# One core of a hybrid streaming encoder step: value chunks, gate sums, weight loads and the first output tiles moved between stages of the even layer

## What is computed

```python
def even_layer(...):
    h = rmsnorm(x, g_pre)
    proj = jnp.einsum('bld,de->ble', h, w_in)
    u, v, za, zb, xbc, dt_raw = jnp.split(proj, EVEN_SPLITS, axis=-1)
    ya, v_rows = gmlp_branch(u, v, za, ws, bs, gv)         # silu(z) * gelu(u) * (W @ rmsnorm(gelu(v)) + b)
    yb, s_fin, new_ctx = ssd_branch(zb, xbc, dt_raw, ...)  # Mamba-2 scan, silu(zb) gate, rmsnorm over 2 groups
    o = jnp.einsum('ble,ed->bld', jnp.concatenate([ya, yb], axis=-1), w_out)
    return x + rmsnorm(o, g_post), v_rows, s_fin, new_ctx
```

## Time and profile before

| | us |
|---|---|
| median of 3 runs | 1649.04 (1648.13 to 1650.0) |
| the profiled execution, device time | 1649.58 |
| its span | 1647.8 |
| PE busy | 1573.0 (95%) |
| PE weight loads busy | 1448.2 (88%) |
| DVE, ACT, POOL busy | 795.8 (48%), 664.1 (40%), 439.5 (27%) |
| DMA | 121.08 MB, 73 GB/s over the span |
| TensorE granted clock, mean | 0.989 |

### The profile page before, as it was taken

One profiled execution on the slowest core, in us unless ns is written; L12 is line 12 of the kernel. 1 busy time (PEld: TensorE's weight loads), 2 busy tenths in 40 slices (PEclk: granted clock), 3 DMA queues, 4 the chain that ended last, 5 costly groups with the idle time before them and its releaser, 6 DMA issues.

```text
span 1647.8 us, 26614 instructions
## 1 busy us (share of the span) xinstructions
PE 1573.0 (95%) x9539; PEld 1448.2 (88%) x9539; DVE 795.8 (48%) x1752; ACT 664.1 (40%) x1241; POOL 439.5 (27%) x267
## 2 busy tenths in 40 slices
PE   6999999998999999999998899999999999998898
PEld 5999999998999999888887888889888889887676
DVE  5547776674883412236475533443344343435432
ACT  6433332331233323335455344544454544445321
POOL 1214543442211112144342221312221221215000
PEclk9999999999999999999999899999999999999999
DMA  4122232112102111154454446624142423213121
GB/s 147 41 67 70 58 92 64 56 44 78 42 13 68 39 38 40 49 179 153 166 177 135 59 73 43 64 53 67 33 71 45 65 39 64 58 42 134 52 90 71
DMA packets 129221, 121.08 MB, mean 73 GB/s; under 512 B 10074, under 2 KB 112996, under 8 KB 129164
## 3 DMA queue, kind: packets, MB, share of 16 engines
q1 hardware_dynamic: 129164, 120.31, 29.9%
HBM read 101.63 MB, written 18.66 MB: 73 GB/s over the span
## 4 chain that ended last, share of the span: by engine, by line
PE 82%; DVE 6%; issue 5%; ACT 5%; DMA 1%; POOL 1%; ACTq 0%; SPq 0%; DVEq 0%; POOLq 0%
PE PB L727 77%; PE PB L731 5%; DVE NRML L1850 2%; ACT L1290 1%; ACT L1736 1%; ACT NRMH L1284 1%; DVE SB L1854 0%; ACT SB L1813 0%; DMA nf_rows<-NFROW 0%; ACT WH L1284 0%; POOL WL L612 0%; ACT PT L1284 0%; ACT SQJ L1324 0%; DVE XT L1857 0%; DVE KALL L1857 0%
## 5 line engine op out<-in xcount | busy, mean ns | idle before, releaser
L727 PE MATMUL PB<-HH,WH 128*128 128x352 f32 x1872 | 621.3, 332 | 8.5 <-ACT VG L1304 4.3
L727 PE MATMUL PB<-HH,WL 128*128 128x352 f32 x1872 | 604.1, 323 | 0.0
L727 PE MATMUL PB<-HL,WH 128*128 128x352 f32 x1872 | 603.5, 322 | 0.0
L727 PEld LDWEIGHTS PB<-HH,WH 128*128 128x128 f32 x1872 | 354.2, 189 | 22.7 <-issue 13.9
L727 PEld LDWEIGHTS PB<-HL,WH 128*128 128x128 f32 x1872 | 355.3, 190 | 0.0
L727 PEld LDWEIGHTS PB<-HH,WL 128*128 128x128 f32 x1872 | 353.8, 189 | 0.0
L612 POOL TENSOR_TENSOR WL<-WRAW,WH 128x1024 fp32r<-128x1024 f32 x82 | 200.2, 2441 | 552.4 <-ACT WH L1284 544.8
L1284 ACT ACTIVATE WH<-WRAW 128x1024 fp32r<-128x1024 f32 x112 | 117.9, 1053 | 28.1 <-DMA WRAW<-in_w_in_even_dram 19.2
L1813 ACT ACTIVATE SB<-SB,small 128x128 f32<-128x128 f32 (+8 forms) x72 | 53.8, 748 | 80.5 <-DVE small L1854 80.5
L1850 DVE TENSOR_TENSOR Y<-PB,Y 128x128 f32 (+2 forms) x72 | 20.2, 280 | 132.5 <-PE PB L727 132.5
L727 PE MATMUL PB<-PT,VTOK 128*128 128x128 f32 (+2 forms) x624 | 81.7, 274 | 0.1
(11 more groups left out here) (299 smaller groups left out, 2396.8 us busy)
## 6 DMA issues: line engine op xcount, KB each, us to landing
WRAW<-in_w_out_even_dram SPq DMA_DIRECT2D x48, 512.0 KB, 3.5
WRAW<-in_w_in_even_dram SPq DMA_DIRECT2D x44, 512.0 KB, 3.8
WRAW<-in_w_in_odd_dram SPq DMA_DIRECT2D x32, 512.0 KB, 8.1
ACSB<-acs_rows SPq DMA_DIRECT2D x16, 528.0 KB, 4.8
NFB<-nf_rows SPq DMA_DIRECT2D x8, 656.0 KB, 3.8
XS<-in_x_prompt_dram SPq DMA_DIRECT2D x8, 512.0 KB, 7.1
XT<-in_x_prompt_dram SPq DMA_DIRECT2D x8, 512.0 KB, 5.2
x_rows<-OG SPq DMA_DIRECT2D x8, 512.0 KB, 5.4
```

What stands on the lines that cost most here:

```text
L727: return pe.matmul(out, lhsT, rhs, start=start, stop=stop)
```

## The change

Four parts, all in the even layer:

- **The last pair.** PE projects a chunk in steps 0, 1, 3 and 5: the three of value tile 21, then the first of tile 22. ACT reads tile 21's chunks (`read_v`) within the pair and makes the high part of tile 23 there. Of the two remaining chunks of tile 22 one stands ahead of the turn of `CST`, one behind it. SP loads tiles 23 and 24 ahead of the store of `CSO`.
- **Tiles 31 and 32** are loaded ahead of the wait for `V` and the store of its sample rows.
- **The gate sums** go two by two behind the three chunks of tile 32, into banks 6 and 7 by turns; the copy of `VS` for the next spatial product moves ahead of their reads on DVE.
- **The first output tiles.** ACT's `prepare(0)` and `prepare(1)` stand ahead of the reads of the last two tiles (43 and 44), DVE's `lows(0)` and `lows(1)` ahead of the last `gated`.

```diff
@@ SP
+        for j in range(2):
+            load_w(tile_no(W_V + 2 + j, 1, 0), even(D + P * j + 2 * P))
         sp.wait_ge(S("cso"), 1)
...
-        with sp.Fori(1, 4) as i:
+        with sp.Fori(2, 4) as i:
             for j in range(2):
                 load_w(tile_no(W_V + j, 2, i), even(D + P * j + 2 * P * i))
         load_w(tile_no(W_UZ, 1, 0), even(0))
         load_w(tile_no(W_UZ, 1, 1), even(2 * D))
+        load_w(tile_no(W_UZ + 2, 1, 0), even(P))
+        load_w(tile_no(W_UZ + 3, 1, 0), even(2 * D + P))
         sp.wait_ge(S("v_normed"), 4)
...
-        with sp.Fori(1, 8) as t:
+        with sp.Fori(2, 8) as t:
@@ PE, pair_steps
-                elif i in (1, 3, 5):
-                    project_chunk(tile_no(W_V, 1, 0), tile_no(W_V, 1, 0), i // 2, HH, HL)
+                elif i in (0, 1, 3):
+                    project_chunk(tile_no(W_V, 1, 0), tile_no(W_V, 1, 0), (0, 1, 1, 2)[i], HH, HL)
+                elif i == 5:
+                    project_chunk(tile_no(W_V + 1, 1, 0), tile_no(W_V + 1, 1, 0), 0, HH, HL)
@@ PE, v_group
-        pe.wait_ge(S("yf"), 24)
-        turn(PB[3][0:6 * XBC_TILES, 0:P], CST[:, :, :].rearrange("p r t -> p (r t)")).then_inc(S("cst_turn"), 1)
-
...
-            if not isinstance(i, int):
+            if isinstance(i, int):
+                project_chunk(vt[1], vt[1], 1, HH, HL)
+                pe.wait_ge(S("yf"), 24)
+                turn(PB[3][0:6 * XBC_TILES, 0:P], CST[:, :, :].rearrange("p r t -> p (r t)")) \
+                    .then_inc(S("cst_turn"), 1)
+                project_chunk(vt[1], vt[1], 2, HH, HL)
+            else:
                 project(vt[0], vt[0], HH, HL)
-            project(vt[1], vt[1], HH, HL)
+                project(vt[1], vt[1], HH, HL)
@@ PE, the gate sums
-        project_uz(0, 1)
-
-        pe.wait_ge(S("s_read"), 3)
-        for n in range(6):
-            g, c = n // 3, n % 3
-            pe.wait_ge(S("y_sq"), 4 + 4 * g)
-            if n == 5:
-                pe.wait_ge(S("gs_ms"), 1)
-            mm(PB[(3, 4, 5, 6, 7, 3)[n]][:, 0:CH], ONES[:, :], RSY[:, g, c * CH:(c + 1) * CH]).then_inc(S("gs_mm"), 1)
-        pe.wait_ge(S("gs_ms"), 6)
+        u1, z1 = tile_no(W_UZ + 2, 1, 0), tile_no(W_UZ + 3, 1, 0)
+        project(u1, u1, HH, HL)
+        for c in range(3):
+            project_chunk(z1, z1, c, HH, HL)
+            for n in (2 * c, 2 * c + 1):
+                pe.wait_ge(S("y_sq"), 4 + 4 * (n // 3))
+                if n >= 2:
+                    pe.wait_ge(S("gs_ms"), n - 1)
+                mm(PB[6 + n % 2][:, 0:CH], ONES[:, :], RSY[:, n // 3, n % 3 * CH:(n % 3 + 1) * CH]) \
+                    .then_inc(S("gs_mm"), 1)
         spatial(0, 1)
@@ ACT
+                if not project and i == 2:
+                    read_v(0)
+                    read_v(1)
+                if not project and i == 3:
+                    read_v(2)
+                    split_high(tile_no(W_V + 2, 1, 0))
...
+        def read_v(c):
+            act.wait_ge(S("p_chunk"), times(tile_no(W_V, 1, 0), 3, c + 1))
+            act.activation(VG[:, c * CH:(c + 1) * CH], PB[c][:, 0:CH], ACT.Gelu).then_inc(S(f"c_read{c}"), 1)
...
-        with order.loop(2, 8, 0) as t:
+        with order.loop(2, 7, 0) as t:
             act.wait_ge(S("ya"), t)
             read_uz(t)
-        load_ln_exp()
...
+        act.wait_ge(S("ya"), 7)
+        prepare(0)
+        prepare(1)
+        read_uz(7)
+        load_ln_exp()
...
         act.wait_ge(S("yb_normed"), 8)
-        prepare(0)
-        prepare(1)
@@ DVE
+        move_v(0, 0)
         gated(0, 0)
+        move_v(0, 1)
         for n in range(6):
             g, c = n // 3, n % 3
-            dve.wait_ge(S("gs_mm"), 3 * g + 3 if n < 5 else 6)
+            dve.wait_ge(S("gs_mm"), n + 1)
...
+        normalise_yb(2, 0)
+        move_v(3, 0)
+        gated(3, 0)
+        normalise_yb(6, 1)
+        move_v(3, 1)
...
         lows(0)
         lows(1)
+        gated(3, 1)
```

More of the change, by code:

```diff
@@ L1504, in inverse_root, with read_group @@
             act.activation(x, x, ACT.Exp, scale=-0.5).then_inc(S(done), 1)
-        with order.loop(0, 4, 0) as i:
-            act.wait_ge(S("v_turn"), 6 * i)
+        def read_group(i):
             for j, out in enumerate((VG, UG)):
+                if j == 0 and isinstance(i, int):
+                    continue
                 w = tile_no(W_V + j, 2, i)
@@ L1513, in _ @@
             act.activation(GSM[:, 2, 0:9], GSM[:, 2, 0:9], ACT.Sqrt).then_inc(S("v_rt"), 1)
+        read_group(0)
+        with order.loop(1, 4, 0) as i:
+            act.wait_ge(S("v_turn"), 6 * i)
+            read_group(i)
         def row_root(out, x, done):
@@ L2116, in _, with move_v @@
         dve.wait_ge(S("gv_stored"), 16)
+        def move_v(i, j):
+            wait(dve, "s_mm", 6 * i + 3 * j)
+            dve.tensor_copy(VS[:, :, :], V[:, 2 * i + j, :].rearrange("p (b f) -> p b f", f=P)).then_inc(S("vs"), 1)
         def gated(i, j):
             t = 2 * i + j
-            wait(dve, "s_mm", 6 * i + 3 * j)
-            dve.tensor_copy(VS[:, :, :], V[:, t, :].rearrange("p (b f) -> p b f", f=P)).then_inc(S("vs"), 1)
             dve.wait_ge(S("c_read2"), W_UZ + 2 + 4 * i + 2 * j)
@@ L2138, in normalise_yb @@
                 ALU.mult, ALU.mult).then_inc(S("yb_normed"), 1)
+        move_v(0, 0)
         gated(0, 0)
+        move_v(0, 1)
         for n in range(6):
             g, c = n // 3, n % 3
-            dve.wait_ge(S("gs_mm"), 3 * g + 3 if n < 5 else 6)
-            ts(RSY[:, g, c * CH:(c + 1) * CH], PB[(3, 4, 5, 6, 7, 3)[n]][:, 0:CH], 1.0 / 512, EPS, ALU.mult, ALU.add) \
+            dve.wait_ge(S("gs_mm"), n + 1)
+            ts(RSY[:, g, c * CH:(c + 1) * CH], PB[6 + n % 2][:, 0:CH], 1.0 / 512, EPS, ALU.mult, ALU.add) \
                 .then_inc(S("gs_ms"), 1)
@@ L2149, in _ @@
         normalise_yb(7, 1)
-        with order.loop(1, 4, 2) as i:
+        with order.loop(1, 3, 2) as i:
             for j in range(2):
                 normalise_yb(4 * j + i - 1, j)
+                move_v(i, j)
                 gated(i, j)
+        normalise_yb(2, 0)
[3 more added lines that the diff above has]
+        move_v(3, 1)
         def lows(u):
```

## The result

The changed kernel took 1639.08 us (median of 4 runs, 1638.46 to 1640.53) where the kernel before, beside it, took 1649.16: a ratio of 0.994 (0.9923 to 0.9958), some 10 us. The forecast was 1634.0, with a range of 1630 to 1638.5: the sign was right, but 10 us came where 15.6 were forecast, and the time lies just outside the range. The profiled execution took 1639.51 us (span 1637.4). PE does the same work in a shorter span.

A forecast was written before the change was run, and what follows sets the result against it. PE, busy 95% of the span, was taken as the bound, with time to gain only from its gaps and lower-clock stretches. 4.0 + 2.2 + 3.9 + 5.5 = 15.6 us off 1649.58 gave 1634.0, range 1630 to 1638.5.

The forecast's parts named there:

- so the gain should arrive at the end whole: Behind 700 us, to the kernel's end: none of the 15.6 us gained earlier would be lost.
- all waits hang on PE or on what PE starts: Behind 700 us: the ground given for the whole 15.6 us reaching the end.
- The second rival: Falls of parts 3 and 4 return elsewhere, or early output units wait for weight loads: 1635.7 to 1639; chance 0.18.
- last sign of being wrong: Odd layer: the forecast is wrong if that layer's stretch is not of the length it had.
- Part 1: End of the SSD pairs: 5.7 us gained, less 1.7 for a fall behind a new 5.3 us gap; net 4.0.
- The first rival: New wait at UG: parameters land sooner, DVE's memsets end it; Part 1 nets 7.2, time 1630.8; chance 0.15.
- Part 2: Tiles 31 and 32: earlier loads remove the 2.2 us gap, no clock share; 2.2, between 1.5 and 2.4.
- Part 3: Gate sums: spreading them removes a 2.2 us wait and the fall behind it; 3.9, between 2.0 and 4.0.
- part 4: First output tiles: earlier splitting removes a 3.8 us gap and its 1.7 fall; 5.5, between 2.8 and 5.6.
- The check: Time from tile 23's first chunk to unit 0's first matmul: 288.7 us before, 280.5 forecast.
- Rival 3: Value groups: another engine sets the pace, PE waits again; chance 0.05 between 1639 and 1645.7, 0.03 for no change.
- Rival 4: Last pair: slower if tile 23's load lands late, delaying CSO; gain gone at 404.6, 1653 at 408; chance 0.03.

The follow-up runs named there:

- Experiments 2: Changed kernel with DVE's wait for the gate parameters moved from ahead of all value groups to the product that reads them: 1631.68 us.
- experiment 3: Changed kernel with DVE clearing V's rows and making group 0's copies ahead of its waits for stores and parameters and the RSY memset: 1629.25 us.
- Experiments 4: As experiment 3, with DVE's wait for the store of V's rows moved behind the first copy of VS: 1628.57 us, 0.987 of the kernel before.
- 7: Changed kernel with the six gate sums in a row again, the copy of VS left where the change put it: 0.9944 of the kernel before.
- 16: Kernel before with the last gate sum multiplied three more times, 1.8 us more work: 1649.98 us, ratio 0.9993.
- 8: Changed kernel with the first two y tiles split behind the last product again: median 4.06 us over a repeat of the changed kernel.
- experiment 6: Changed kernel with the loads of tiles 31 and 32 behind the store of V's rows again: 0.9940 of the kernel before.
- experiment 13: Changed kernel with the last gate sum multiplied four more times, 2.4 us of extra work: median moved by 1.3 us.

## Why the prediction was wrong

The gaps of the four parts went as forecast, and the new one came where it was forecast. One sentence failed, one cost was put at nothing, and one was mis-sized.

- **The step that failed: "so the gain should arrive at the end whole".** Of 13.99 us at the first turn of `XT`, 10.4 arrived in the profiles, and 10.1 in the medians. The last head has idle of 2.65, 2.6 and 1.97 us (for `NRML`, `KALL` and `YL`), and whether and for how long the clock falls behind each differs between profiles: the length is 73.7 to 73.9 us with two falls of 3.4, 74.2 and 74.5 with three, and 76.3 to 76.9 where 6.8 us at half the clock stand behind the idle for `KALL` and 3.4 behind that for `YL`, in 19 profiles of 15 kernels. The profile of before had the good pattern, that of after the bad one. Its premise, "all waits hang on PE or on what PE starts", leaves out the clock and two things more: a fall can be free where PE would wait for POOL anyway (the 1.14 us for `WOL`), and an instruction of DVE can be slowed by one of POOL. That is head 0, as far as its rows tell: 86.0 to 86.3 us against 85.4, with the 1.22 us of DVE in all 12 long ones. All 12 are among the 14 profiles of the changed kernel and its variants, and none among the 5 of the old order; what decides it is open. The second rival named falls that come back, but only up to the first output units, not 700 us later. The prediction's own last sign of being wrong, an odd layer not of the length it had, is the one that came.
- **Part 1, "Net 4.0": 3.1, or 2.9 by its undoing.** The gap was 5.65 for 5.3: `WS` was issued at 394.0 and landed at 400.9, so tile 23 started 5.2 us sooner and not 5.7. The fall was 6.8 us long and cost 2.1, not the 1.7 I subtracted; the earlier trace rows has just this case behind the gap of 4.26, at 2.1, and I used it as a bound only. Experiments 2 and 3 show the wait, the landing behind it and its price: 5.2 to 8 us lay there to be had. The first rival did not come: `WS` landed 6.9 us after its issue.
- **Part 2, "2.2, between 1.5 and 2.4": 1.3.** I costed the earlier low part of tile 31 at nothing. It met DVE's `V` products (4.85 us for 2.63), made the store late and cost 0.87 us; the rows at 420 us in the trace of the kernel before had the price. Experiments 4 and 6 cut that chain at either end.
- **Part 3, 3.9: 4.0** in the pair of profiles, and **part 4, 5.5: 5.6.** By undoing: 1.7 and 6.3. (The bound of 2.8 for part 4 with the fall kept doesn't follow from its terms; the gap alone is 3.8.) The gaps were sized rightly both times (2.19, of which 0.7 the copy of `VS`; 3.80); the share of the clock is none behind the sums in 7 and 16, 1.7 in the kernel before, and 2.4 in 8 (6.8 us with PE at work in 4.9), so it is luck that it came out at the forecast's 1.7 both times.
- **The check** from the first chunk of tile 23 to unit 0 was 280.5; it is 683.42 - 401.96 = 281.5. Rival 3 (DVE paces the value groups) falls by experiment 3, where PE is 8 us earlier still and never waits for DVE there. Rival 4 did not occur: `CSO`'s turn came at 390.03 for 389.8. (The longest median of the page before is 9.2 us, a load of `POSTF`, and not 8.1; nothing hangs on it.)

Of the clock the runs show falls behind gaps of 1.88 us (experiment 13, at 944 us), 1.97 (last head, after), 2.01 (experiment 6) and 3.80 (8), and none behind others of 2.61 (2), 2.65 (last head, after) and 1.48 (7). The Trainium skill (TensorE: Matmul & The Clock Gate, "HAM oscillation") would have the clock stay for all but the one of 3.8; experiment 6, 0.50 behind a gap of 2.01, speaks against it here. In three executions of the changed kernel the fall around the last turn of `UG` began 2.6, 3.0 and 1.6 us ahead of that turn, so it is not tied to the gap. The same page has the watch run free of the kernel; these three agree, while three equal last heads in three profiles, for each of the two kernels, do not look like a free draw.

**Still open.** How much the mean of many runs loses in the last head by an earlier or later start. Without the last head's 2.8 us and head 0's 0.9 the two profiles would differ by 14 us, the medians differ by 10 to 11, so on the mean of many runs the two kernels may still differ there. The delays move the medians by 0.8, 1.3 and 3.5 us for 1.2, 2.4 and 3.4 of work, and in the kernel before by -0.9 and 2.7 for 1.8 and 3.6: a median does not simply rise by the work, but four to eleven runs a kernel don't give the curve.

## What to carry to other kernels

A gap of PE costs itself and, in some executions, up to 3 us of lost work at half the clock (6.8 us with PE busy in 6.1 in the last head), or nothing, where PE would only have waited for another engine a little later. So sum the gaps, keep the clock's share apart as a range, and let that range reach to every gap of some 2 us and more (1.88, in experiment 13, was the shortest with a fall behind it here) down to the end of the kernel, edited or not. When an engine's work moves earlier, look at what the other engines run there: the price of the meeting of POOL and DVE stood in the trace of before. When work is packed closer, ask of the engine that waits whether it waits for what it reads or only for what stands ahead of it: here three parameters, a memset and a store stood ahead of copies that needed none of them, and moving the waits brought as much (10.3 us in the median, 9.1 at `XT`) as the change itself.

## What the runs showed of the hardware

- DVE and POOL hold each other up. Two `TENSOR_TENSOR` of 128x1152 took 4.85 us beside POOL's `WL` product and 2.63 without it; POOL's took 3.46 and, in experiment 6, 2.34. Alone they sum to 4.97, and together they were done 4.85 us after the first began: one after the other, as far as the sums tell, not side by side. The Trainium skill (SBUF — State Buffer, "SBUF: two separate sides") says so of DVE instructions with two SBUF inputs: the pair of ports is an exclusive lock; the rows agree.
- A delay can be free: with 1.8 us more of matmuls ahead of a gap the time did not change (0.9993, 0.9983 to 1.0002).
- A fall of the clock can be free: in the last head, 3.4 us, 6.8 us or none at half the clock behind the first idle, and the turn of `KALL` at 20.3 to 20.5 us each time, since PE otherwise waits 1.14 us for POOL and longer for DVE.
